# A two-block transformer kernel: w_o by halves of its rows, fill units among the recurrence's turns, and other engines' orders around them

## What is computed

```python
og = gla_chunked(qg, kg, vg, log_a)                 # recurrence in chunks of 64
o_gla = rms_norm(og, g_gla_out) * silu(r_gla)
o_mem = attention of q_mem over the 256 memory rows  # 4 heads
o_mla = causal_block_attention(q_full, k_full, v_mla) # 8 heads, keys from w_ukv
gates = sigmoid(gate_logits + b_gate)                # three branches
y = gates[0] * o_mla + gates[1] * o_gla + gates[2] * o_mem
x = x + y @ w_o
h2 = rms_norm(x, g_ffn)
return x + square(relu(h2 @ w_up)) @ w_down
```

## Time and profile before

| | |
|---|---|
| median of 3 runs | 967.76 us (965.82 to 968.11) |
| the profiled execution | 966.22 us |
| its span | 964.6 us |
| PE busy | 920.7 us, 95% of the span, 4684 instructions |
| DVE busy | 734.5 us, 76% |
| ACT busy | 531.8 us, 55% |
| POOL busy | 159.1 us, 16% |
| chain that ended last | PE 74%, DVE 13%, ACT 7%, issue 4% |
| mean granted clock of PE | 0.99 of full speed |

### The profile page before, as it was taken

The page is one execution under the profiler, slowest core; times in us unless marked ns, Lnnn a source line. Parts: engine busy times, 40 slices in busy tenths (PEclk is TensorE's granted clock), DMA queues, the critical chain, the costliest instruction groups (busy, mean ns, idle before and its releaser), DMA issues.

```text
span 964.6 us, 13743 instructions
## 1 busy us (share of the span) xinstructions
PE 920.7 (95%) x4684; PEld 737.9 (76%) x4684; DVE 734.5 (76%) x1048; ACT 531.8 (55%) x809; POOL 159.1 (16%) x247
## 2 busy tenths in 40 slices
PE   6999999998989799999999999999999899999996
PEld 5787787786867587888888888666677688888885
DVE  5787556878566777888677878876568879999977
ACT  6566664465765545555533344666574676666631
POOL 8000000124600000011011100480000014444400
PEclk9999999998999999999999999999999999999998
DMA  8674634776552334888678956332225555555571
GB/s 257 229 229 150 195 111 132 239 267 203 164 164 77 110 120 153 266 271 265 209 250 301 335 168 205 119 98 87 78 94 170 195 155 174 175 176 181 181 252 58
DMA packets 100035, 175.12 MB, mean 182 GB/s; under 512 B 8284, under 2 KB 36476, under 8 KB 99980
## 3 DMA queue, kind: packets, MB, share of 16 engines
q1 hardware_dynamic: 92748, 148.87, 48.4%
q0 software_dynamic: 7184, 25.50, 8.0%
q10 hardware_dynamic: 48, 0.04, 0.0%
HBM read 173.33 MB, written 1.05 MB: 181 GB/s over the span
## 4 chain that ended last, share of the span: by engine, by line
PE 74%; DVE 13%; ACT 7%; issue 4%; DMA 1%; DVEq 0%; SPq 0%; ACTq 0%
PE acc L735 61%; DVE wlo L1821 4%; ACT whi L1340 2%; PE turned L1205 1%; PE scores L1194 1%; PE turned L828 1%; DMA raw<-in_w_mem_kv 1%; PE turned L1306 1%; PE scores L974 1%; PE turned L771 1%; DVE turn L1876 1%; PE turned L1094 1%; PE turned L940 1%; PE turned L1117 1%; DVE arena L2260 1%
## 5 line engine op out<-in xcount | busy, mean ns | idle before, releaser
L1821 DVE TENSOR_TENSOR wlo<-raw,whi 128x1024 fp32r<-128x1024 f32 (+2 forms) x270 | 344.0, 1295 | 93.5 <-ACT whi L1340 83.6
L1340 ACT CAST whi<-raw 128x1024 fp32r<-128x1024 f32 (+2 forms) x270 | 273.7, 1030 | 181.3 <-PE acc L735 133.6
L735 PE MATMUL acc<-whi,lta_lo 128*128 128x512 f32 (+2 forms) x576 | 230.8, 401 | 7.8 <-DVE lta_lo L1861 6.6
L735 PE MATMUL acc<-wlo,lta_hi 128*128 128x512 f32 (+2 forms) x576 | 223.1, 387 | 0.0
L735 PE MATMUL acc<-whi,lta_hi 128*128 128x512 f32 (+2 forms) x576 | 222.7, 387 | 0.0
L735 PEld LDWEIGHTS acc<-whi,lta_lo 128*128 128x128 f32 x576 | 108.7, 189 | 45.0 <-issue 14.1
L735 PEld LDWEIGHTS acc<-wlo,lta_hi 128*128 128x128 f32 x576 | 108.7, 189 | 22.5
L735 PEld LDWEIGHTS acc<-whi,lta_hi 128*128 128x128 f32 x576 | 108.9, 189 | 19.2
L735 PE MATMUL acc<-whi,ltb_lo 128*128 128x512 f32 (+1 forms) x272 | 108.2, 398 | 5.0 <-DVE ltb_lo L2599 2.4
L642 POOL DMA_DIRECT2D wm<-in_w_mod x48 | 34.5, 720 | 464.3 <-DVEq L1921 267.5
L735 PE MATMUL acc<-wlo,ltb_hi 128*128 128x512 f32 (+1 forms) x272 | 105.0, 386 | 0.0
(11 more groups left out here) (348 smaller groups left out, 1322.5 us busy)
## 6 DMA issues: line engine op xcount, KB each, us to landing
raw<-in_w_in SPq DMA_DIRECT2D x88, 512.0 KB, 3.9
wm<-in_w_mod POOLq DMA_DIRECT2D x48, 512.0 KB, 5.4
raw<-in_w_up SPq DMA_DIRECT2D x88, 256.0 KB, 3.0
raw<-in_w_up SPq DMA_DIRECT2D x32, 512.0 KB, 4.7
raw<-in_w_down SPq DMA_DIRECT2D x32, 512.0 KB, 5.0
raw<-in_w_down SPq DMA_DIRECT2D x44, 256.0 KB, 3.2
raw<-in_w_mem_kv SPq DMA_DIRECT2D x8, 512.0 KB, 5.3
raw<-in_w_o SPq DMA_DIRECT2D x8, 512.0 KB, 3.9
```

Source lines behind the costliest of these rows:

```text
L735: ins = pe.matmul(acc[s][:, t, 0:n], lhs[part][:, kt0 + kk, tok], w[:, u % RING, kk, 0:n], start=(k == 0 and kk == 0 and j == 0), stop=(la ...
L1340: act.copy(whi[:, s, :, 0:n], raw[:, s, :, 0:n]).then_inc(hi_ready, 1)
L1821: dve.tensor_tensor(wlo[:, s, :, 0:n], raw[:, s, :, 0:n], whi[:, s, :, 0:n].bitcast(F32), ALU.subtract)\
```

## The change

Four things move, and one panel pair is cut another way. The amount of PE's work on weights stays: eight units of w_o, and so on.

1. **Panels of w_o.** WO0 and WO1 (four units each) become WOA0, WOA1, WOB0, WOB1 (two units each). A takes slices 0 to 3 of the mixed rows (channels 0 to 511), B slices 4 to 7, so that both output halves receive their first part before the second half of the mixed rows is needed; B goes on in the bank where A has left its sum (`opens`, `closes`). The turns of y.0 and y.1 move into the last MLA pair, ahead of its O; y.2 comes behind the first and y.3 behind the second unit of WOA1. `mix(1)` becomes `mix_pair(2)` and `mix_pair(3)` of 256 columns. `hc` is turned behind WOB0.1 and behind WOB1.0.
2. **Gates and fill in MLA.** `mla_units` is 1, 3, 5, 7, 8. The gate of G11 stands ahead of the attention, that of G00 at pair 1, that of G01 at the last pair behind y.0 and y.1.
3. **The recurrence's begin.** Units Q1.0 and Q1.1 run behind the turns gqT and gkT, not behind the scores of step 0. DVE's memset and first exponents and ACT's first exponential stand ahead of the weighing of the last but one memory head.
4. **The recurrence's end and the turns of the keys.** At s = 8 DVE does the modulation row and the weights ahead of the split and the bias add; PE runs UKV0 ahead of `go`; ACT takes G21's sigmoid and the four `go` outputs ahead of `sqrt("qq")`. kn.1 and kn.3 are taken out by DVE; `gate("G10")` stands behind qn.0.

```diff
@@ names and tables
-    out += [("WO0", KT, 1), ("WO1", KT, 1), ("CX", KT, 2)]
+    out += [(f"WO{h}{c}", KT // 2, 1) for h in "AB" for c in range(2)] + [("CX", KT, 2)]
-    return (1, 3, 4, 6, 8)[min(j, MLA_PAIRS)]
+    return (1, 3, 5, 7, 8)[min(j, MLA_PAIRS)]
-    out += pairs_t("MLA", MLA_PAIRS)
-    out += g("y", 4) + g("hc", 4) + g("h2", 4)
+    out += pairs_t("MLA", MLA_PAIRS, ahead={MLA_PAIRS - 1: g("y", 4)[:2]})
+    out += g("y", 4)[2:] + g("hc", 4) + g("h2", 4)
@@ PE
-            for name, src in (("gqT", gq), ("gkT", gk)):
+            qg = ["Q1", "Q2", "G20", "G21"]
+            for j, (name, src) in enumerate((("gqT", gq), ("gkT", gk))):
                 turn_tokens(name, src, 4)
+                fill(qg, j, 1)
...
-                if s < 8:
+                if 1 <= s < 8:
                     fill(qg, 2 * s, 2)
...
+            pe.wait_ge(ev("ckT_ready"), 1)
+            unit("UKV0", 0, ckT)
             for name in ("gla.off", "gla.7.0", "gla.7.1"):
...
+                if p == MLA_PAIRS:
+                    turn_mixed((0, 1), 1)
...
-            turn_tokens("y", r_gla, ready="branches_mixed", groups=(0, 1))
-            for k in range(4):
-                if k == 1:
-                    turn_tokens("y", r_gla, ready="branches_mixed", groups=(2, 3))
-                lt_wait("y", k)
-                unit("WO0", k, lta)
+            for c in range(2):
+                for k in range(2):
+                    lt_wait("y", k)
+                    unit(f"WOA{c}", k, lta)
+                    if c == 1:
+                        turn_mixed((2 + k,), 2 + k)
             pe.wait_ge(ev("ctx_landed"), 16)
-            for k in range(4):
-                if k % 2 == 0:
-                    turn_tokens("hc", ar(8192, T, D), groups=(k, k + 1))
-                unit("WO1", k, lta)
+            for c in range(2):
+                for k in range(2):
+                    lt_wait("y", 2 + k)
+                    unit(f"WOB{c}", k, lta, first_kt=KT // 2 + UNIT * k)
+                    if c != k:
+                        turn_tokens("hc", ar(8192, T, D), groups=(2 * c, 2 * c + 1))
@@ ACT
+            gla_exponentials(1)
             b, k = T_USE[f"MEM.O{H_MEM - 1}"]
...
-            sqrt("qq", stat[:, 4:6, :])
+            gate("G21")
             for t in range(T):
                 for g in range(2):
                     t_out(f"go.{2 * t + g}", og[:, t, 2 * g:2 * g + 2, :].rearrange("p a b -> p (a b)"))
+            sqrt("qq", stat[:, 4:6, :])
...
-            for g in range(4):
+            for g in (0, 2):
                 t_out(f"kn.{g}", knT[:, 2 * g:2 * g + 2, :].rearrange("p a b -> p (a b)"), scale=col("g_k_nope"))
+            gate("G11")
@@ DVE
+            def recurrence_begins(i):
+                if i == H_MEM - 1:
+                    done(dve.memset(attn, 0.0))
+                    exponents(1)
...
                 if s < 8:
                     exponents(s + 1)
+                else:
+                    mod_row(3)
+                    weights(8)
                 ahead(u0 + 2 * s)
...
             mod_out(3)
-            weights(8)
...
+            ahead(PLAN.unit["G00"])
+            for g in (1, 3):
+                b, k = T_USE[f"kn.{g}"]
+                dve.wait_ge(t_full[b], k + 1)
+                dve.tensor_scalar(knT[:, 2 * g:2 * g + 2, :].rearrange("p a b -> p (a b)"), tb[b][:], col("g_k_nope"), None,
+                                  ALU.mult).then_inc(t_free[b], 1)
+            gate_in_psum("G11")
...
+            def mla_between(p):
+                if p == 0:
+                    gate_on("G11", r_gla)
+                    done(dve.tensor_tensor(r_gla, r_gla, o_mem, ALU.add))
+                elif p == MLA_PAIRS - 1:
+                    lt_dve("y", lta, groups=(0, 1))
...
+            def mix_pair(p):
+
+                b, k = T_USE[f"MLA.O{p}"]
                 dve.wait_ge(t_free[b], k + 2)
-                gate_on(f"G0{c}", o_mla)
+                dve.wait_ge(gate_sig, n_gate["G01"] + 1)
+                first = 256 * (p % 2)
+                part = slice(256 * p, 256 * p + 256)
+                ins = dve.tensor_tensor(o_mla[:, :, part], o_mla[:, :, part],
+                                        acc[PLAN.bank("G01")[0]][:, :, first:first + 256], ALU.mult)
+                if p == MLA_PAIRS - 1:
+                    frees("G01", ins)
+                    dve.sem_inc(panel_out[PLAN.bank("WOA1")[0]], 1)
+                else:
+                    done(ins)
...
-            lt_dve("y", lta, groups=(0, 1))
-            mix(1)
-            lt_dve("y", lta, groups=(2, 3))
+            ahead(PLAN.unit["WOA0"] + 1)
+            for g in (2, 3):
+                mix_pair(g)
+            for k in range(2):
+                ahead(PLAN.unit["WOA1"] + k)
+                lt_dve("y", lta, groups=(2 + k,))
```

More of the change, by code:

```diff
@@ L996, in _ @@
                     ins.then_inc(full, 1)
-            pe.wait_ge(ev("ckT_ready"), 1)
-            for c in range(4):
+            for c in range(1, 4):
                 unit(f"UKV{c}", 0, ckT)
@@ L1590, in mla_after @@
             def mla_after(p):
-                if p in (0, 1, 3):
-                    gate(("G11", "G00", "G01")[(p + 1) // 2])
+                if p == 1:
+                    ahead(PLAN.unit["G00"] + mla_units(p) + 1)
+                    gate("G00")
+                elif p == MLA_PAIRS - 1:
+                    lt_act("y", lta, (0, 1))
+                    gate("G01")
             attend_pairs("MLA", MLA_PAIRS, mla_exps, PLAN.unit["G00"], mla_units, 3, after=mla_after)
-            lt_act("y", lta)
-            ahead(PLAN.unit["WO1"])
+            for k in range(2):
+                ahead(PLAN.unit["WOA1"] + 1 + k)
+                lt_act("y", lta, (2 + k,))
+            ahead(PLAN.unit["WOB1"])
             lt_act("hc", ltb, (0, 1))
-            ahead(PLAN.unit["WO1"] + 1)
+            ahead(PLAN.unit["WOB1"] + 1)
             lt_act("hc", ltb, (2, 3))
@@ L2228, in exponents @@
                 ins.then_inc(gla_exp, 1)
+            def recurrence_begins(i):
+                if i == H_MEM - 1:
+                    done(dve.memset(attn, 0.0))
+                    exponents(1)
+            u0 = PLAN.unit["V1"]
+            attend("MEM", H_MEM, mem_maxima, sums2,
+                   lambda i, r, bank: weigh2(o_mem[:, :, DV_MEM * i:DV_MEM * i + DV_MEM], bank, r, DV_MEM),
+                   lambda i: u0 + 4 * max(i - 1, 0), lambda i: u0 + min(4 * i + 2, 14), mem_after,
+                   before_weighing=recurrence_begins)
+            u0 = PLAN.unit["Q1"]
+            ahead(u0)
+            dve.wait_ge(ev("gmask_ready"), 1)
             def decayed(s):
@@ L2330, in mla_maxima @@
                 return neg(s, 2, (NOPE + ROPE) ** -0.5)
+            def mla_between(p):
+                if p == 0:
+                    gate_on("G11", r_gla)
+                    done(dve.tensor_tensor(r_gla, r_gla, o_mem, ALU.add))
+                elif p == MLA_PAIRS - 1:
+                    lt_dve("y", lta, groups=(0, 1))
             def mla_after(p):
                 if p == 1:
-                    gate_on("G11", r_gla)
-                    done(dve.tensor_tensor(r_gla, r_gla, o_mem, ALU.add))
+                    ahead(PLAN.unit["G00"] + mla_units(p) + 1)
+                    gate_in_psum("G00")
                 elif p == 2:
-                    mix(0)
-                if p in (0, 1, 3):
-                    gate_in_psum(("G11", "G00", "G01")[(p + 1) // 2])
-            def mix(c):
-                part = slice(COLS * c, COLS * c + COLS)
-                b, k = T_USE[f"MLA.O{MLA_PAIRS // 2 * (c + 1) - 1}"]
-                dve.wait_ge(t_free[b], k + 2)
-                gate_on(f"G0{c}", o_mla)
+                    b, k = T_USE["MLA.O1"]
+                    dve.wait_ge(t_free[b], k + 2)
+                    gate_on("G00", o_mla)
+                    dve.sem_inc(panel_out[PLAN.bank("WOA0")[0]], 1)
+                    part = slice(0, COLS)
+                    done(dve.tensor_tensor(r_gla[:, :, part], r_gla[:, :, part], o_mla[:, :, part], ALU.add))
+                    dve.sem_inc(ev("branches_mixed"), 1)
+                elif p == MLA_PAIRS - 1:
+                    gate_in_psum("G01")
+            def mix_pair(p):
+                b, k = T_USE[f"MLA.O{p}"]
+                dve.wait_ge(t_free[b], k + 2)
+                dve.wait_ge(gate_sig, n_gate["G01"] + 1)
[8 more added lines that the diff above has]
+                    done(ins)
                 done(dve.tensor_tensor(r_gla[:, :, part], r_gla[:, :, part], o_mla[:, :, part], ALU.add))
@@ L2355, in mla_weigh @@
                 return ins
-            attend_pairs("MLA", MLA_PAIRS, mla_maxima, sums_of_pair, mla_weigh, PLAN.unit["G00"], mla_units, mla_after)
-            lt_dve("y", lta, groups=(0, 1))
-            mix(1)
-            lt_dve("y", lta, groups=(2, 3))
+            attend_pairs("MLA", MLA_PAIRS, mla_maxima, sums_of_pair, mla_weigh, PLAN.unit["G00"], mla_units, mla_after,
+                         before_weighing=mla_between)
```

(8 more changed lines are left out.)

53 lines of the change are left out of this document (29 added, 24 removed).

## The result

The changed kernel takes 970.97 us (median of 16 runs, 967.36 to 972.29), the kernel before 966.31 beside it (16 runs, 964.99 to 968.11): a ratio of 1.0043, 95% interval 1.0033 to 1.0052. It is 4 us slower. The forecast was 969.0 in a range of 963.0 to 973.5, so the range holds the time; but the likeliest case was "no change" (966 to 970.6), and what came is the slower rival, 971.5. The 969.0 also flatters the forecast: it stood on a median of three runs of the kernel before, 967.76, which is 1.45 above the 966.31 measured beside the changed kernel. As a change, +1.2 was forecast and +4.2 came. The profiled execution takes 971.57.

What follows compares the result with a forecast made beforehand. PE, busy 95% of the span, was taken as the bound, so only its waits and slow clock count: -1.6 - 1.3 + 2.2 + 2.1 - 2.5 = -1.1, +2.3 for one clock fall, +1.2: 969.0 us, range 963.0 to 973.5.

Steps and rivals of the forecast that it cites:

- the likeliest case: Whole kernel: the forecast case, 969.0 us, own range 966 to 970.6, all within 0.3% of no change; chance 0.42.
- the slower rival: Both waits over 3 us (UKV3, WOA1) stand in full, clock falls at all three places: +3.8, 971.5 us; chance 0.32.
- Place 1: Memory attention to recurrence: earlier first exponentials and moved Q1 units cut PE's waits, -1.6 us (bounds -2.0 and 0).
- Place 2: Recurrence to kv panels: two old waits go, new ones of 1.4 and 3.3 us at UKV2 and UKV3; -1.3 us.
- the last term of the sum: UKV3 and WOA1: one of these two waits over 3 us lowers PE's clock, +2.3 us.
- the upper bound: Recurrence to kv panels: +1.1 us if the clock is down over the wait at UKV3.
- Place 3: Turned keys for MLA: a serial chain to kn.3 idles PE 3.85 + 0.85 us; net +2.2, plus +2.1 for the clock.
- the credit for waits that go: Turned keys: old waits of 0.34 + 0.82 and part of some 1.0 for qn.2 set against the new idle time.
- Place 4: MLA's end, w_o, CX: 8.9 us of waits and 3.0 of slow clock go, 7.4 + 2.0 come; -2.5 us.
- kn's fall: Turned keys: the clock falls behind the 4.7 us idle, 2.5 less 0.4 taken up in PT1, +2.1 us.
- it doesn't do what it says: Recurrence's end: go products start no sooner, step 8's weights still wait for scores; 971.0 us, counted with the slower case.

Runs made afterwards that it cites:

- mix_first: Changed kernel with DVE doing G01's bias add ahead of the split before it and the second split behind the two mixes: 965.79 us, R 1.0001 to the kernel before.
- xadd_first: Changed kernel with DVE adding the second half of w_o's output to x right behind hc.3's scaling: 967.14 us, R 1.0027 to the kernel before.
- kn_early: Changed kernel with DVE taking kn.1 and kn.3 out ahead of the third split instead of behind it: 965.53 us, R 0.9994 to the kernel before.
- kn_act: Changed kernel with all four kn outputs on ACT again: 964.19 us, R 0.9983 to the kernel before.
- root_early: Changed kernel with ACT's root for the queries ahead of the four go outputs: 965.08 us, R 0.9990 to the kernel before.
- wo_only: Kernel before with all edits but the recurrence's (turns of the keys, MLA's gates, w_o halves): 971.74 us, R 1.0057 to the kernel before.
- all_four: Changed kernel with kn.1 and kn.3, the root, the mix and the x add all moved earlier: 951.46 us, R 0.9857 to the kernel before.
- halves_only: Kernel before with only MLA's gates and the w_o halves as changed: 966.37 us, R 1.0014 to the kernel before.
- five: all_four with kn all on ACT, and y.0 and y.1 copied ahead of the last pair's second split: 951.65 us.

## Why the prediction was right and where it was wrong

*Place 1* was right to 0.1 us: -1.64. The cover was there, no wait for ACT remains in front of the scores; one of 0.7 us for step 0's weights took its place, against the 0.35 allowed.

*Place 2's* waits were right: 1.33 forecast as 1.4, 3.16 as 3.3, POOL first. The step that failed is the last term of the sum, "of the two further waits over 3 us … I expect one to lower it". The clock fell here too, from 246.7 to 253.6, which is why the place gave +1.8 and not -1.3: PE worked at half speed for 6.0 us of it, 3.0 us lost, and -1.3 + 3.0 is 1.7. I had this as the upper bound, put at +1.1. Two kernels with the same instructions and the same 3.2 us wait at UKV3 show the price apart from the wait: in the profiled executions of `mix_first` and `xadd_first` the clock did not fall there, and G10's first product came at 250.25 and 250.43, where it is 252.81 in the changed kernel.

*Place 3* was right as a mechanism, confirmed by `kn_early` and `kn_act`. Its size was 4.3 and is 5.6: idle 3.63 + 0.89, as the 3.85 + 0.85 of the forecast, but the credit for waits that go was put at 2.5 and was 1.6 (0.8 gained ahead of the kn turns, and the 0.82 ahead of the scores; the 0.34 stays), and nothing of the 2.5 us for the clock was absorbed in PT1, whose wait is 0.57 now, before 0.48.

*Place 4*: WOA1's wait of 3.55 is 3.30, O3's 1.35 is 1.65, h2's 2.0 is 2.55. The chains were right; both clock falls behind them (345.7 to 349.1 and 376.4 to 379.9, half of 6.9 us) were not in the -2.5, and the second was in no case of mine. With them the sum would have been +0.9 and the place measured -0.4; where the 1.3 us between went stays open.

So the likeliest case was wrong in one term above all, how often PE's clock falls: it had kn's fall and one of two others, and the profiled execution has four, the fourth at h2. The slower rival was right in its places, three long waits in full and a fall behind each. That its +3.8 comes so near to the +4.2 is partly luck: it had nothing for the fall at h2 (1.7 us), it priced the falls at UKV3 and WOA1 at 2.4 and 2.5 where 3.0 and 1.7 were lost, place 3 cost 1.3 more than its 4.3, the 1.3 us that stay open at place 4 went the other way, and the profiled +5.3 is itself above the +4.2 of the runs. I had weighed it at 0.32, below the no-change case, though its condition (waits over 3 us, all longer than the 2.17 us piece that had lowered it before) was met three times over on my own sum. The forecast took kn's fall in and split the difference between the other two. The rival "it doesn't do what it says" fell: the go products started at 231.87 and not 234.02, at full clock, 0.5 us of it beyond what place 1 had given, with a unit of UKV0 done ahead of them.

## What to carry to other kernels

When a reordering takes a wait out, write down for each engine what stands behind the moved instruction and when the busiest one gets it; here all four losses were one instruction (a split, a root, a bias add, an x add) on the wrong side of another, and four moves turned +4 us into -14 us. Price every wait of PE as long as these (2.2 us and more) with the slow clock behind it, in full, and carry the case without it as the rival: it fell behind most of them here, not behind all, and from run to run of one kernel it differs. And test a bundle of edits apart: the recurrence's part had a gain of some 6 us in it, hidden by the place of one root.

## What the runs showed that was not expected

The clock is not a function of one wait, and not of the kernel alone. The fourteen profiled executions, by place (waits in us; a fall is a window with a granted clock of 0.50 behind the wait):

| place | wait | profiled kernels with it | clock fell in |
|---|---|---|---|
| weights of step 8, order of before | 2.2 | 4 | 4 |
| ahead of WO0, order of before | 5.0 | 3 | 3 |
| kn.3 and first scores, late | 3.6 and 0.9 | 5 | 5 |
| the same, early | 0.2 to 0.6 and 0.9 | 2 | 1 |
| ahead of WOA1 | 3.3 | 7 | 6 |
| UKV3 | 3.2 | 6 | 4 |
| h2's turns | 2.5 to 2.6 | 7 | 4 |

With the same wait, the clock fell in one kernel and not in the other, and a longer wait was not the surer one: those of 2.2 us had a fall behind them in four of four, those of 3.2 in four of six. The length of the fall differs too: behind kn.3 the clock was low for some 7 us in the changed kernel and in `root_early`, for some 10 in `mix_first`, `xadd_first` and `wo_only`.

Nor do two executions of one kernel agree, as the mean granted clock of every run shows. The clearest case is `kn_act`: its profiled execution took 966.05 us at 0.990, with falls behind UKV3, WOA1 and h2, and its fastest run 960.69 at 0.998, as much as `all_four` has, whose profile shows no fall in this stretch. The same instructions, with three waits of 2.5 to 3.3 us in their order, can thus run nearly without a fall. In `halves_only` and `kn_act` time and clock go together run by run (correlation -0.91 in both), so most of their spread of 5.4 us is the clock's. It is not all there is to spread: `all_four` lies within 1.2 us in 4 runs, but `five`, without a wait over 1.4 us in that stretch, still spreads over 2.3 us in 4 runs, at 0.997 to 0.998. What decides in a single run whether the clock falls, no run here shows.
